# Hybrid decoder trunk on one core: the conv channels' input projection with the weight tiles stationary, the normed x 64 bytes off a multiple of 128

## The reference: what is computed

```python
h = rms_norm(x, attn_norm_w[l])
proj = h @ w_in[l]
q, k, v, z, xbc, dt_raw = jnp.split(proj, SPLIT_POINTS, axis=-1)
attn = sliding_window_attention(q, k, v, q_norm_w[l], k_norm_w[l], sinks[l])
ssm = mamba2_mixer(z, xbc, dt_raw, conv_w[l], conv_b[l], ...)   # silu(causal_depthwise_conv(xbc)) first
x = x + concat([attn, ssm]) @ w_out[l]
h = rms_norm(x, ffn_norm_w[l])
x = x + (silu(h @ w_gate[l]) * (h @ w_up[l])) @ w_down[l]
```

## Time and profile before

| what | value |
|---|---|
| three runs | 2175.59, 2175.71, 2176.92 us, median 2175.71 |
| the profiled execution | 2175.55 us, span 2173.7 us (1.85 us lie outside the span) |
| granted TensorE clock, mean | 0.999 of full speed |
| PE busy | 2160.9 us, 99% |
| DVE busy | 1176.4 us, 54% |
| ACT busy | 1000.8 us, 46% |
| POOL busy | 112.7 us, 5% |
| DMA | 392.16 MB, 180 GB/s |

### The profile page before, as it was taken

The page is one execution under the profiler, slowest core; times in us unless marked ns, Lnnn a source line. Parts: engine busy times, 40 slices in busy tenths (PEclk is TensorE's granted clock), DMA queues, the critical chain, the costliest instruction groups (busy, mean ns, idle before and its releaser), DMA issues.

```text
span 2173.7 us, 25034 instructions
## 1 busy us (share of the span) xinstructions
PE 2160.9 (99%) x10150; PEld 1791.7 (82%) x10150; DVE 1176.4 (54%) x1382; ACT 1000.8 (46%) x1292; POOL 112.7 (5%) x157
## 2 busy tenths in 40 slices
PE   9999999999999999999999999999999999999999
PEld 7888888888888888888888888888888888888887
DVE  5866765445544455444467667554544445444443
ACT  5555654444444444434445556444444444443332
POOL 2023100000000000000000222000000000000000
PEclk9999999999999999999999999999999999999999
DMA  7554356666666665555556543566666666656664
GB/s 219 174 165 134 117 174 187 193 193 188 191 187 191 191 190 189 187 195 192 189 165 180 155 134 119 184 184 193 192 188 189 188 192 189 189 190 203 202 200 134
DMA packets 202850, 392.16 MB, mean 180 GB/s; under 512 B 12224, under 2 KB 12592, under 8 KB 202736
## 3 DMA queue, kind: packets, MB, share of 16 engines
q1 hardware_dynamic: 201952, 388.67, 58.3%
q0 software_dynamic: 784, 1.90, 0.4%
HBM read 388.43 MB, written 2.10 MB: 180 GB/s over the span
## 4 chain that ended last, share of the span: by engine, by line
PE 98%; ACT 1%; issue 0%; POOL 0%; SPq 0%; DMA 0%; DVE 0%; DVEq 0%; ACTq 0%
PE ps L484 91%; PE ps L493 3%; PE ps L586 1%; PE ps L535 0%; PE ps L649 0%; PE ps L650 0%; PE ps L622 0%; PE ps L623 0%; PE ps L648 0%; POOL ys L451 0%; DMA vrows<-in_k_norm_w_dram 0%; PE ps L594 0%; PE ps L591 0%; PE ps L577 0%; ACT w_hi L807 0%
## 5 line engine op out<-in xcount | busy, mean ns | idle before, releaser
L1047 DVE TENSOR_TENSOR w_lo<-raw,w_hi 128x1024 fp32r<-128x1024 f32 x736 | 907.0, 1234 | 864.1 <-ACT w_hi L807 862.9
L807 ACT CAST w_hi<-raw 128x1024 fp32r<-128x1024 f32 x736 | 772.2, 1049 | 945.9 <-PE ps L484 941.0
L484 PE MATMUL ps<-w_hi,h_hi 128*128 128x512 f32 x1984 | 622.6, 395 | 0.0
L484 PE MATMUL ps<-w_hi,h_lo 128*128 128x512 f32 x1984 | 612.2, 390 | 0.0
L484 PE MATMUL ps<-w_lo,h_hi 128*128 128x512 f32 x1984 | 611.3, 389 | 0.0
L484 PEld LDWEIGHTS ps<-w_lo,h_hi 128*128 128x128 f32 x1984 | 372.4, 188 | 78.9
L484 PEld LDWEIGHTS ps<-w_hi,h_lo 128*128 128x128 f32 x1984 | 372.3, 188 | 78.8
L484 PEld LDWEIGHTS ps<-w_hi,h_hi 128*128 128x128 f32 x1984 | 365.9, 188 | 70.9 <-DVE w_lo L1047 0.7
L484 PE MATMUL ps<-w_hi,f_hi 128*128 128x512 f32 x960 | 297.5, 391 | 0.0
L484 PE MATMUL ps<-w_hi,f_lo 128*128 128x512 f32 x960 | 295.8, 389 | 0.0
L484 PE MATMUL ps<-w_lo,f_hi 128*128 128x512 f32 x960 | 295.7, 389 | 0.0
(11 more groups left out here) (183 smaller groups left out, 822.4 us busy)
## 6 DMA issues: line engine op xcount, KB each, us to landing
raw<-in_w_gate_dram SPq DMA_DIRECT2D x176, 512.0 KB, 4.4
raw<-in_w_up_dram SPq DMA_DIRECT2D x176, 512.0 KB, 3.7
raw<-in_w_down_dram SPq DMA_DIRECT2D x176, 512.0 KB, 3.6
raw<-in_w_in_dram SPq DMA_DIRECT2D x144, 512.0 KB, 3.6
raw<-in_w_out_dram SPq DMA_DIRECT2D x64, 512.0 KB, 3.8
out_dram<-xr SPq DMA_DIRECT2D x4, 512.0 KB, 5.1
xr<-in_x_dram POOLq DMA_DIRECT2D x3, 512.0 KB, 5.7
xr<-in_x_dram SPq DMA_DIRECT2D x1, 512.0 KB, 4.5
```

What stands on the lines that cost most here:

```text
L484: done = nc.tensor.matmul(ps[:, bank + t, :], lhs[:, rows + k, t * P:(t + 1) * P], w[:, slot, k, :], start=(first and k == 0 and w is w_hi ...
L807: nc.scalar.copy(w_hi[:, slot, :, :], raw[:, slot, :, :]).then_inc(hi_split, 1)
L1047: v_.tensor_tensor(w_lo[:, slot, :, :], raw[:, slot, :, :], w_hi[:, slot, :, :].bitcast(F32), ALU.subtract).then_inc(lo_split, 1)
```

## The change

`products_turned` replaces `products` for groups 0 to 3: a 128 x 128 tile of the weights is stationary and 256 tokens of h move, so that the result is channels by tokens at once; a pair takes 24 matmuls of 256 columns in place of 12 of 512. `conv_in` goes (its eight transposes, four times a layer), and so do the four evacuations by ACT. Since tokens now lie along the row, the factor per token must too: `spread_rs` turns `rs`, broadcast along its row, by two transposes after pair 8 (bank 7), ACT copies that to `rsb` (`rsb_out`, at p = 8), and DVE multiplies a whole group (128 x 1024) by it on the way from PSUM to `stage` (`channels`, at p = 9, 15, 23, 31). `conv` then reads `stage` in SBUF in place of PSUM. `turn_dt` waits for `rsb_ready` too, since it writes the same bank. The counts of `act_evac` follow. The 64-byte tensor `ea` moves ahead of `h_hi`, so that `h_hi` and `h_lo` start 64 bytes off a multiple of 128; `stage` and `ident` come to lie 64 bytes off one as well, and `wdt_s` on one.

```diff
+        ea = sb("ea", [P, HS])
+        h_hi = sb("h_hi", [P, KT, TOK], F32R, 64)
+        h_lo = sb("h_lo", [P, KT, TOK], F32R, 64)
+        rsb = sb("rsb", [P, TOK])
...
-            def conv_in(layer, j):
-                pe.wait_ge(act_evac, layer * G_IN + (j + 1))
-                if j:
-                    pe.wait_ge(tok_ready, layer * 3 + j)
-                else:
-                    pe.wait_ge(h_lo_ready, layer * 16 + 8)
-                turned(4, chunk_tiles(lambda t: stage[:, j % 2, t, :]), ch_psum)
+            def products_turned(slot, pair, rows, bank, first, last):
+
+
+                pe.wait_ge(lo_split, pair + (1 + RING))
+                for k in range(2):
+                    for m in range(CT):
+                        for h, w in ((h_hi, w_hi), (h_lo, w_hi), (h_hi, w_lo)):
+                            done = nc.tensor.matmul(ps[:, bank + m // 2, m % 2 * TOK:(m % 2 + 1) * TOK],
+                                                    w[:, slot, k, m * P:(m + 1) * P], h[:, rows + k, :],
+                                                    start=(first and k == 0 and w is w_hi and h is h_hi and m % 2 == 0),
+                                                    stop=(last and k == 1 and w is w_lo), skip_group_check=True)
+                done.then_inc(pair_used, 1)
+
+            def spread_rs(layer):
+                pe.wait_ge(rs_ready, layer * 2 + 1)
+                for t in range(T):
+                    last = nc.tensor.transpose(ps[:, 7, t * P:(t + 1) * P], rs[:, t:t + 1].broadcast_to([P, P]),
+                                               ident[:, :])
+                last.then_inc(rsb_psum, 1)
...
             def turn_dt(layer):
                 pe.wait_ge(dtT_ready, layer + 1)
+                pe.wait_ge(rsb_ready, layer + 1)
...
-                    if g >= 2:
-                        pe.wait_ge(act_evac, layer * G_IN + (g - 1))
+                    if g >= 6:
+                        pe.wait_ge(act_evac, layer * 5 + (g - 5))
+                    elif g >= 2:
+                        pe.wait_ge(ch_ready, layer * 4 + (g - 1))
...
-                        if 8 <= p < 40 and p % 8 == 0:
-                            conv_in(layer, p // 8 - 1)
+                        if p == 8:
+                            spread_rs(layer)
...
+            def rsb_out(layer):
+                act.wait_ge(rsb_psum, layer + 1)
+                nc.scalar.copy(rsb[:, :], ps[:, 7, 0:TOK]).then_inc(rsb_ready, 1)
...
+                    if p == 8:
+                        rsb_out(layer)
-                    if p % 8 == 7 and p < 63:
+                    if p % 8 == 7 and 32 < p < 63:
                         evacuate(layer, p // 8)
...
+            def channels(layer, j):
+
+                if j == 0:
+                    dve.wait_ge(rsb_ready, layer + 1)
+                dve.wait_ge(pair_used, layer * PAIRS + ((j + 1) * PPG + RING))
+                at = in_bank(layer, j)
+                v_.tensor_tensor(by_tile(stage[:, j % 2]), by_tile(ps[:, at:at + 2, :]),
+                                 rsb[:, :].unsqueeze(1).broadcast_to([P, CT, TOK]), ALU.mult).then_inc(ch_ready, 1)
+
             def conv(layer, j, m):
 
-                dve.wait_ge(ch_psum, layer * 4 + (j + 1))
-                u = ps[:, 4 + m // 2, m % 2 * TOK:(m % 2 + 1) * TOK]
+                if m == 0:
+                    dve.wait_ge(ch_ready, layer * 4 + (j + 1))
+                    if j:
+                        dve.wait_ge(tok_ready, layer * 3 + j)
+                u = by_tile(stage[:, j % 2])[:, m, :]
...
+                    if p == 9 or 15 <= p < 32 and p % 8 == 7:
+                        channels(layer, p // 8 - 1 if p == 9 else p // 8)
                     if 9 <= p < 37 and p % 8 in (1, 2, 3, 4):
                         conv(layer, p // 8 - 1, p % 8 - 1)
```

More of the change, by code:

```diff
@@ L122, in hybrid_decoder @@
         xr = sb("xr", [P, T, D], F32, 512)
-        h_hi = sb("h_hi", [P, KT, TOK], F32R, 512)
-        h_lo = sb("h_lo", [P, KT, TOK], F32R, 512)
+        ea = sb("ea", [P, HS])
+        h_hi = sb("h_hi", [P, KT, TOK], F32R, 64)
+        h_lo = sb("h_lo", [P, KT, TOK], F32R, 64)
+        rsb = sb("rsb", [P, TOK])
         stage = sb("stage", [P, 2, T, N])
@@ L160, in hybrid_decoder @@
         dt = sb("dt", [P, T, HS])
-        ea = sb("ea", [P, HS])
         cums = sb("cums", [P, 3, HS])
@@ L236, in hybrid_decoder @@
         cum_psum, cum_ready, ecum_ready = sem("cum_psum"), sem("cum_ready"), sem("ecum_ready")
-        ch_psum, conv_ready, silu_ready = sem("ch_psum"), sem("conv_ready"), sem("silu_ready")
+        rsb_psum, rsb_ready = sem("rsb_psum"), sem("rsb_ready")
+        ch_ready, conv_ready, silu_ready = sem("ch_ready"), sem("conv_ready"), sem("silu_ready")
         tok_psum, tok_ready = sem("tok_psum"), sem("tok_ready")
@@ L448, in gate @@
                     part = slice(z * N, (z + 1) * N)
-                    pool.wait_ge(act_evac, layer * G_IN + (8 + z))
+                    pool.wait_ge(act_evac, layer * 5 + (4 + z))
                     pool.wait_ge(y_ready, layer * 8 + 8)
@@ L695, in _ @@
                             pe.wait_ge(h_lo_ready, layer * 16 + (q + 1))
-                        products(q % RING, base + p, 2 * q, in_bank(layer, g), h_hi, h_lo, q == 0, q == PPG - 1)
+                        if g < 4:
+                            products_turned(q % RING, base + p, 2 * q, in_bank(layer, g), q == 0, q == PPG - 1)
+                        else:
+                            products(q % RING, base + p, 2 * q, in_bank(layer, g), h_hi, h_lo, q == 0, q == PPG - 1)
                         if layer == 0 and p in (0, 2):
@@ L727, in _ @@
                     if n < 2:
-                        pe.wait_ge(act_evac, layer * G_IN + (G_IN - 1 + n))
+                        pe.wait_ge(act_evac, layer * 5 + 4 + n)
                     else:
@@ L850, in evacuate @@
                 act.wait_ge(pair_used, layer * PAIRS + ((g + 1) * PPG + RING))
[L851 to L854, removed]
+                if 4 <= g < 6:
+                    act.wait_ge(conv_ready, layer * 4 + (g - 1))
                 if g == 6:
@@ L1123, in cum_out, with by_tile @@
                     .then_inc(cpart_ready, 1)
-            def conv(layer, j, m):
-                dve.wait_ge(ch_psum, layer * 4 + (j + 1))
-                u = ps[:, 4 + m // 2, m % 2 * TOK:(m % 2 + 1) * TOK]
+            def by_tile(v):
+                return v.rearrange("p b (a c) -> p (b a) c", a=2)
+            def channels(layer, j):
[5 more added lines that the diff above has]
+                                 rsb[:, :].unsqueeze(1).broadcast_to([P, CT, TOK]), ALU.mult).then_inc(ch_ready, 1)
+            def conv(layer, j, m):
+                if m == 0:
[3 more added lines that the diff above has]
+                u = by_tile(stage[:, j % 2])[:, m, :]
                 tile_ = CT * j + m
```

## The result

The changed kernel takes 2206.46 us (median of 4 runs, 2206.03 to 2206.97) against 2175.68 for the one before: a ratio of 1.014, with 95% interval 1.0123 to 1.0158. It is 30.8 us slower, and the predicted range ended at 2178.5. The profiled execution has a span of 2205.2 against 2173.7, at a granted clock of 0.999 of full speed (the 2.4 GHz level) as before.

A forecast was written before the change was run, and what follows sets the result against it. PE, busy 99% of the span, was taken as the bound. A layer: -3.56 (conv_in) + 0.25 (spread_rs) + 1.12 (wait) = -2.19, both -4.4, giving 2171.3 us; range 2168.8 to 2178.5.

The forecast's parts named there:

- point 1: Products step: 32 pairs a layer go from 12 wide to 24 narrow matmuls, a pair staying 2.72 us; cost 0.
- The fifth: Rival: xr transposes slow at the new distance to ident, 1 to 2 us; counted within the fixed-cost rival's 0.15.
- the 118 that I had kept as a bound: Narrow products: upper bound of 118 ns a matmul for a stream that does not settle, 7.2 us more.
- the 114 that the prediction names as a sign of being wrong: Narrow products: the prediction is wrong if their pace is above 114 ns a matmul.
- no fixed cost: Narrow against wide products: both take 0.443 ns a column, two narrow ones cost what a wide one does.
- the one new wait: PE at conv_out of group 0, released by ACT's silu: some 1.1 us in both layers, none in groups 1 and 2.
- `conv_in` was worth 7.1 us: PE loses four conv_in a layer, each eight transposes costing 0.89 us: -3.56 a layer.
- the 2.2 of the sum: PE's waits for silu at conv_out of group 0, 1.12 and 1.11 us in the two layers.
- the split of pair 12 in layer 0: ACT's split behind the new copy: start at 43.69 in place of 43.57, 0.12 later.
- the rival of that name: Rival of no wait at conv_out: 2169.1 us, needing channels far below 1.21 us; chance 0.08.
- the forecast's -4.4: Whole kernel: -2.19 us a layer from conv_in, spread_rs and the new wait, both layers -4.4 us.

The follow-up runs named there:

- e2: The kernel before, with only h_hi and h_lo moved to 64 bytes off a multiple of 128: 2211.43 us, ratio 1.0164.
- e3: The changed kernel with w_hi, w_lo and xr also 64 bytes off a multiple of 128, f staying on: 2185.50 us, ratio 1.0046.
- e1: The changed kernel with h_hi and h_lo back at a multiple of 128 bytes: 2179.46 us, ratio 1.0018.
- e5: Changed kernel, h back on a multiple of 128, weight ring slots 4160 bytes, only conv pairs' weights 64 off: 2200.23 us, ratio 1.0113.

## Why the prediction was wrong

**The step that failed** stands at the end of point 1: "The 512-wide products now read a stationary h at the new offset; one load in 226.7 ns leaves slack for that: 0." It measured 6.7 ns on each matmul, 0.080 us on each of 432 pairs, 34.6 us at most, of which the span shows some 31 (27.3 in the gate and up projections). e2 has this edit alone and its loss alone; e3 takes the distance away and the loss with it. The error of thought was to look at how much of the time a load takes, where the question was how it is placed beside the moving stream. The moved tensor was judged by the products that the diff rewrites, and 432 pairs in lines that it leaves alone read it too. No rival had it. The fifth came nearest, with slower transposes of `xr` at the new distance to `ident`; those did not happen, they stay 109 ns apart in before, after and e2.

**The pace of the narrow products**, "I take 113.3, since the new stream is long and of one kind, and the offsets are alike": 117.8 in most pairs, near the 118 that I had kept as a bound, and above the 114 that the prediction names as a sign of being wrong. The bound held at this distance, though not at 0, where e1 has 120.0; the choice did not. That a stream settles after six matmuls is no rule. `dt_products` in the earlier trace rows does, with nothing interrupting it. In after its 32 matmuls of layer 0, at the same 64 or 192 bytes of distance within 256, stay slow to the end:

```profile
37.58 0.28 PE L549 MATMUL ps<-h_hi,wdt_s 128*128 128x256 f32 x1
...
41.24 0.28 PE L549 MATMUL ps<-h_lo,wdt_s 128*128 128x256 f32 x1
```

That is 3.66 us for 31 distances, 118.1 ns each.

**That the earlier trace rows show no fixed cost** was a confounded comparison. In the earlier trace rows both tiles start at the same place within 512 bytes, in the earlier trace rows they are 64 or 192 apart within 256. At equal distance 0 (e1) a wide matmul takes 226.7 ns and a narrow one 120.0: over the columns at 2.4 GHz, 213.3 and 106.7, that is 13.3 ns in both. The price of halving the columns is that, on 768 more matmuls, 10.2 us, and e1 has it. The Trainium skill has this in kind (TensorE: Matmul & The Clock Gate, Back-to-back issue gap): columns over 2.4 GHz and 2.5 ns for each matmul, which by the same section is the gap without the load's share, too low for few columns where each matmul has its own load. The prediction left that condition out. From the 2.5 ns one would get an estimate of 1.9 us; the measurement, 13.3 ns, decides.

**What held.** `channels` takes 1216 ns (1.21 foretold), `tensor_scalar` from SBUF 408 (0.13 less than the 538 of the earlier trace rows, as foretold, with two pointer operands). The groups of after, as in the earlier trace rows:

```profile
L1174 DVE TENSOR_SCALAR acc<-stage,vecs 128x256 f32<-128x256 f32 x32 | 13.1, 408 | 0.1
...
L1158 DVE TENSOR_TENSOR stage<-ps,rsb 128x1024 f32<-128x1024 f32 x8 | 9.7, 1216 | 0.1
```

`conv_out` of group 0 is the one new wait, in both layers. ACT's `silu` in layer 1 and PE's timeline around its end, beside the earlier trace rows:

```profile
1155.58 1.06 ACT L898 ACTIVATE acc<-acc 128x1024 f32<-128x1024 f32 x1 [2.44 <-DVE acc L1177]
```

```profile
1155.89 0.28 PE L523 MATMUL ps<-h_hi,w_lo 128*128 128x256 f32 x1
1156.69 1.09 PE L495 MATMUL ps<-ident,acc 128*128 128x128 f32 x8 [0.52 <-ACT acc L898]
```

`silu` ends at 1156.64 and PE starts 0.05 later, as foretold. From the last product to the transposes are 0.80 us where 0.12 is usual, so the wait is 0.7, against 1.12 foretold: PE itself comes later, since its pairs there take 2.83. In layer 0 the same distance is 1.34, a wait of 1.2 against 1.11. The 1.9 together are near the 2.2 of the sum, and groups 1 and 2 have no wait. `spread_rs` and the products around it in layer 0:

```profile
44.07 0.28 PE L523 MATMUL ps<-h_hi,w_lo 128*128 128x256 f32 x1
44.19 0.38 PE L532 MATMUL ps<-ident,rs 128*128 128x128 f32 x2
...
44.53 0.28 PE L523 MATMUL ps<-h_lo,w_hi 128*128 128x256 f32 x1
```

From 44.07 to 44.53 are two products, 0.23 us without the transposes, so these cost 0.23, against 0.25 foretold. That `conv_in` was worth 7.1 us is confirmed only within e1's sum: 3.6 and 0.7 of waits are 4.3, against 4.1 between the spans.

Two figures of the prediction do not follow from its own terms, and neither matters: the split of pair 12 in layer 0 comes out at 43.71 in place of 43.69, and the lower end of the range, 2168.8 for no wait, is 0.3 below the 2169.1 that the rival of that name gives.

The terms in place of the forecast's -4.4: -7.1 for `conv_in`, +0.5, +1.9 for the wait, +5.2 for the narrow pace (49 pairs at 0.107), and 34.6 for h. That is 35.1, and 31.5 measured in the span. Of the difference some 2.9 lie in p = 32 to 71, where 40 pairs a layer lose about 1.75 in place of 3.2 us (the gain of the fourth `conv_in`, at p = 32, taken out), as in e2, and 0.8 in the gate and up projections. Without the term for h the sum is +0.5, some 2176, inside the predicted range though not the gain that was forecast.

**What stays open.** Why distance acts at all. That the load of the next stationary tile and the stream of the moving one get in each other's way in the memory is a guess that no run tests, and it does not say why distance 0 is the best for wide products and the worst for narrow ones. Open too is why the direction matters for wide products (+64 against -64) and not for narrow ones, and what throws a narrow stream from 117.8 to 113.3 ns and back. The period of 256 bytes rests on one distance, 256 itself.

## What to carry to other kernels

When a tensor moves in memory, list every matmul that reads it, not those that the diff rewrites, and read their pace in the timeline before and after: 7 ns on a matmul are invisible in one and are 1.4% of a kernel bound by PE. Judge an offset by its distance to the other operand of the same matmul, and try each shape of product by itself, since what helps 256 columns hurts 512. And before two rows are compared to find a fixed cost, see that they differ in nothing but the size.

## What the runs showed that was not expected

Two tiles that start at the same place within 256 bytes are the best case for 512 columns (226.7 ns against 228.9 to 234.3 elsewhere) and the worst for 256 (120.0 against 113.3 to 118.7). Starting on a multiple of 128 protects nothing: 128 bytes of distance cost a wide matmul 5.7 ns. And the same narrow instructions on the same addresses run at 113.3 or at 117.8 ns. In after they keep one pace until something interrupts them; in e5 and in `dt_products` the pace also falls within an uninterrupted stream.
